# Residual joints of a fused two-layer network on one NeuronCore: norms and the neighbouring product tiles computed in two token halves

## The chip, the cores and the metric

One NeuronCore of one Trainium2 chip. The metric is the device time in microseconds (us) of one execution; the median of several executions is compared.

## The reference

The whole program is a stack of a hybrid mixer layer with cross-attention, a second layer with an attention and recurrence block, a short-convolution mixer, and gated feed-forward blocks, on 512 tokens of width 1024, all in float32. What matters here is the joint between two products of the second part of the stack. With y the output of a projection (1024 features x 512 tokens), h the residual stream, g, g' and s learned or conditioned vectors of 1024 features:

```
h = h + y * rsqrt(mean(y*y) + eps) * g        # first norm, added to the residual
n = h * rsqrt(mean(h*h) + eps) * g' + s       # second norm, input of the next product
z = W_next @ n
```

The means run over the 1024 features of each token. Tokens don't mix here, so any split over tokens is exact. There are four such joints, after the projections ab_out, down_1, sc_out and down_2; after the last one there is only the first line, and h is stored as the result.

## The kernel before

Activations lie feature-major: 128 features on the partitions, KT = 8 feature tiles, 512 tokens along the free axis. A product is computed one output tile of 128 features at a time over all 512 tokens. Each k-step of a tile (one feature tile of the input) is three matmuls in `passes` (lines 393 to 395), because weights and inputs are both split into a rounded high part and a low rest: high x high, high x low, low x high. ab_out has 16 k-steps a tile, down_1 and down_2 have 22, sc_out has 8. Four PSUM banks take the output tiles in turn.

The program is written by hand, engine by engine; each stage gives every engine's queue a list of instructions, and semaphores order them across engines. The weights of a tile come by DMA from SyncE into a ring of six slots; VectorE makes the high part (L344) and the low part (L346), which needs the high slot of the tile three before to be free (`split_until`, `split_weights`).

`plain_product` is the product ahead of a joint. ScalarE squares each output tile from PSUM (L2699) and copies it to y (L2701); GpSimd adds up the squares of the first seven tiles (L419).

`edge` is the joint. TensorE sums the squares over the partitions with a matrix of ones (L473, L476: four blocks of 128 tokens, 128 equal columns each), ScalarE takes the root (L496), VectorE the reciprocal (L518), and TensorE spreads the result over the partitions (`spread_root`, L465). VectorE then scales y (L530) and adds it to h (L534), tile by tile over 512 tokens; ScalarE squares the new h (L508), TensorE sums (L487). After the eighth tile come root, reciprocal and spread again. Then for each tile VectorE scales h (L541), ScalarE adds the shift and rounds it to the high part (L513), and VectorE makes the low part (L547). In between TensorE does `keep_busy` matmuls (L656) into a bank nobody reads: 11, then one after each of seven sums, then 8.

`product` of the next stage takes its first two tiles together (`lead=2`): for each k-step it waits for that tile's low part (`inputs_ready`), then does the three matmuls of tile 0 and of tile 1. The third tile begins when both are done. Behind the joints up_1, sc_in and up_2 follow; behind the last, `store_output` sends each finished tile of h to memory by a DMA from SyncE's queue (L3552). The joint before ab_in is another function, `double_edge`, and the one into up_0 belongs to `ffn_up` and `residual_product`.

Of the kernel before, what the change touches and what calls it, by code (L numbers as in the profile page):

```python
# [32 lines left out]
P = 128  # L33
T = 512
# [187 lines left out]
class Kernel:  # L222
# [126 lines left out]
    def product(self, pe, name, rhs, width, evacuated, between=None, inputs_ready=None, lead=1, banks_free=None,  # L349
                beside=None, upto=None, ready_from=0):  # L350
# [5 lines left out]
        for k in range(kt if lead > 1 else 0):  # L356
            if inputs_ready is not None:
                pe.wait_ge(inputs_ready, k + 1)
            for j in range(lead):
                if k == 0:  # L360
                    if banks_free is not None:
                        pe.wait_ge(banks_free[0], banks_free[1] - PRODUCT_BANKS + j + 1)
                    pe.wait_ge(self.weights_split, first + j + 1)
                last = self.passes(self.psum[:, j % PRODUCT_BANKS, 0:width], first + j, k, rhs(k), k == 0, k == kt - 1)
                if k == kt - 1:
                    last.then_inc(self.weights_used, 1)
            if beside is not None:
                beside(k)
# [18 lines left out]

    def passes(self, out, i, k, x, first, last):
# [11 lines left out]


# [48 lines left out]

def edge(k, name, before, first_gain, gain=None, shift=None, then=None, y=None):
# [3 lines left out]
    squared, added, out = (before.signals[s] for s in ("squared", "added", "out"))  # L455
    summed, rooted, inverted, spread, renewed, resquared, counted, scaled, shifted, steps, done = (
        k.sem(f"{name}_{s}") for s in ("summed", "rooted", "inverted", "spread", "renewed", "resquared", "counted",
                                       "scaled", "shifted", "steps", "done"))
    SUMS, SPREAD = 4, 2
    ones = k.const("ones")  # L460

    def spread_root(pe, i):
        pe.wait_ge(inverted, i + 1)
        for c in range(TT):
            last = nc.tensor.matmul(k.psum[:, SPREAD + i, c * P:(c + 1) * P],  # L465
                                    k.roots[:, i, c:c + 1].broadcast_to([P, P]), k.const("ident"),
                                    start=True, stop=True)
        last.then_inc(spread, 1)

    def tensor(pe):  # L470
        pe.wait_ge(added, KT - 1)
        for c in range(TT):
            nc.tensor.matmul(k.psum[:, SUMS + c, 0:P], k.sum_sq[:, c * P:(c + 1) * P], ones, start=True, stop=False)  # L473
        pe.wait_ge(squared, KT)
        for c in range(TT):
            last = nc.tensor.matmul(k.psum[:, SUMS + c, 0:P], k.squares[:, (KT - 1) % 2, c * P:(c + 1) * P],  # L476
                                    ones, start=False, stop=True)
        last.then_inc(summed, 1)
        spread_root(pe, 0)
        if gain is None:  # L480
            return
        pe.wait_ge(out, KT - 2)
        keep_busy(k, pe, 11)
        for j in range(KT):
            pe.wait_ge(resquared, j + 1)
            for c in range(TT):
                last = nc.tensor.matmul(k.psum[:, SUMS + c, P:2 * P], k.squares[:, j % 2, c * P:(c + 1) * P], ones,  # L487
                                        start=(j == 0), stop=(j == KT - 1))
            last.then_inc(counted, 1)
            if j < KT - 1:  # L490
                keep_busy(k, pe, 1)
        spread_root(pe, 1)
        keep_busy(k, pe, 8)
# [5 lines left out]
    def scalar(act):  # L499
        act.wait_ge(summed, 1)  # L500
        root(act, 0)
        if gain is None:
            return
# [18 lines left out]
    def vector(dve):  # L522
# [13 lines left out]
        if gain is None:  # L536
            return
# [3334 lines left out]
```

## Time and profile before

| | |
|---|---|
| median of 3 runs | 2417.52 us (2414.93 to 2419.92) |
| the profiled execution's own time | 2420.88 us |
| its span, first to last instruction | 2419.1 us |
| mean granted TensorE clock | 0.973 of full speed |
| busy: TensorE matmul, VectorE, ScalarE, GpSimd | 97%, 68%, 27%, 8% of the span |
| matmuls L393 to L395, all products | 722.1 + 712.1 + 712.0 us (inputs in n), 280 us each (inputs in the hidden buffers) |
| read from memory | 247.97 MB, 103 GB/s over the span |

A busy share says how much of the span an engine had an instruction under way. Matmuls overlap: one that is shown with 0.39 us starts 0.23 us after the one before. In the view in order of time a row has the start, the duration, the engine, the line of the code, the operation with output and inputs, and in brackets how long the engine stood idle and what released it. "x8" means eight instructions merged in one row. A float32 matmul of the sums and spreads is two instructions.

### The profile page before, as it was taken

Reading aid. Unit: us, or ns where it says so; the run is one execution under the profiler, and the core shown is the slowest. Engines: PE = TensorE matmul, PEld = TensorE weight load, DVE = VectorE, ACT = ScalarE, POOL = GpSimd, SP = SyncE. Lnnn points to the kernel's source line nnn. Section 1 sums busy time; section 2 is a strip of 40 time slices with the busy share of each in tenths; the row PEclk is TensorE's granted clock in tenths of the full one; section 3 lists DMA queues with packets and bytes.
Section 4 is the critical chain, followed back from the end, with each engine's and each line's share of the span. In section 5 each row is a group of like instructions: output and inputs, shape, how many; then the busy total and the mean of one; then the engine's idle time right before and its main releaser. Section 6 shows DMA issues by size and latency. Waiting matters only on the chain.

```text
span 2419.1 us, 35289 instructions
## 1 busy us (share of the span) xinstructions
PE 2335.3 (97%) x14624; PEld 1898.2 (78%) x14624; DVE 1651.3 (68%) x2569; ACT 663.9 (27%) x1200; POOL 183.2 (8%) x179
## 2 busy tenths in 40 slices
PE   8998879999999999999989999999999999999997
PEld 6886668878888888887756788888888888888886
DVE  6674366756888865559788777666667886666653
ACT  2321253022211201324768413222102113222200
POOL 0001222001000011003211010000010000000000
PEclk9999579999999999999999999999999999999998
DMA  4220003412222453322200361232562451322341
GB/s 183 79 79 2 21 3 122 158 52 88 96 96 96 135 204 130 107 81 92 88 1 2 138 219 62 98 100 97 197 214 104 182 186 63 102 96 96 127 141 64
DMA packets 71728, 253.94 MB, mean 105 GB/s; under 512 B 8560, under 2 KB 8848, under 8 KB 71056
## 3 DMA queue, kind: packets, MB, share of 16 engines
q1 hardware_dynamic: 71280, 251.14, 30.4%
q8 instruction: 116, 1.90, 0.3%
q10 hardware_dynamic: 288, 0.54, 0.1%
q14 instruction: 44, 0.36, 0.0%
HBM read 247.97 MB, written 2.10 MB: 103 GB/s over the span
## 4 chain that ended last, share of the span: by engine, by line
PE 47%; DVE 3%; issue 0%; ACT 0%; POOL 0%; DVEq 0%; POOLq 0%
PE psum L393 14%; PE psum L394 14%; PE psum L395 13%; PE psum L3362 1%; PE psum L487 1%; PE psum L3349 1%; PE psum L3384 1%; DVE scratch L3440 1%; DVE scratch L3416 1%; PE psum L656 0%; PE psum L3376 0%; PE psum L465 0%; DVE h L534 0%; DVE n L530 0%; PE psum L476 0%
## 5 line engine op out<-in xcount | busy, mean ns | idle before, releaser
L393 PE MATMUL psum<-rounded_n,rounded_high 128*128 128x512 f32 x1824 | 722.1, 396 | 8.0 <-DVE rounded_ring L346 4.6
L394 PE MATMUL psum<-rounded_n_low,rounded_high 128*128 128x512 f32 x1824 | 712.1, 390 | 0.0
L395 PE MATMUL psum<-rounded_n,rounded_ring 128*128 128x512 f32 x1824 | 712.0, 390 | 0.0
L346 DVE TENSOR_TENSOR rounded_ring<-ring,rounded_high 128x1024 fp32r<-128x1024 f32 (+1 forms) x360 | 448.4, 1246 | 43.5 <-ACT rounded_high L329 31.5
L393 PEld LDWEIGHTS psum<-rounded_n,rounded_high 128*128 128x128 f32 x1824 | 343.9, 189 | 86.6 <-issue 7.4
L394 PEld LDWEIGHTS psum<-rounded_n_low,rounded_high 128*128 128x128 f32 x1824 | 344.1, 189 | 74.2 <-issue 3.9
L395 PEld LDWEIGHTS psum<-rounded_n,rounded_ring 128*128 128x128 f32 x1824 | 343.7, 188 | 72.1
L344 DVE CAST rounded_high<-ring 128x1024 fp32r<-128x1024 f32 (+1 forms) x347 | 250.4, 722 | 188.3 <-PE psum L395 177.9
L393 PE MATMUL psum<-rounded_arena,rounded_high 128*128 128x512 f32 x720 | 280.2, 389 | 0.0
L395 PE MATMUL psum<-rounded_arena,rounded_ring 128*128 128x512 f32 x720 | 280.1, 389 | 0.0
L394 PE MATMUL psum<-rounded_arena,rounded_high 128*128 128x512 f32 x720 | 280.1, 389 | 0.0
L2617 DVE SCALAR_TENSOR_TENSOR scratch<-arena,vecs,scratch 128x512 f32<-128x512 f32 x88 | 65.9, 748 | 162.8 <-ACT scratch L2604 162.8
L393 PEld LDWEIGHTS psum<-rounded_arena,rounded_high 128*128 128x128 f32 x720 | 135.1, 188 | 28.3 <-issue 0.2
L395 PEld LDWEIGHTS psum<-rounded_arena,rounded_ring 128*128 128x128 f32 x720 | 135.1, 188 | 28.1
L394 PEld LDWEIGHTS psum<-rounded_arena,rounded_high 128*128 128x128 f32 x720 | 135.1, 188 | 27.9
L2598 ACT COPY arena<-psum 128x512 f32<-128x512 f32 x88 | 51.7, 587 | 351.2 <-PE psum L395 351.2
L2604 ACT ACTIVATE scratch<-arena,vecs 128x512 f32<-128x512 f32 x88 | 63.8, 725 | 188.4 <-DVE arena L2638 186.9
L2699 ACT ACTIVATE scratch<-psum 128x512 f32<-128x512 f32 x32 | 19.2, 600 | 317.4 <-PE psum L395 317.4
L419 POOL TENSOR_TENSOR sum_sq<-sum_sq,scratch 128x512 f32<-128x512 f32 x38 | 59.9, 1575 | 288.4 <-ACT scratch L2699 242.2
L416 POOL COPY sum_sq<-scratch 128x512 f32<-128x512 f32 x6 | 4.7, 786 | 955.4 <-ACT scratch L2699 820.0
L993 DVE CUSTOM_DVE_ANT_0 arena<-arena 128x1024 f32<-128x1024 f32 x48 | 61.9, 1333 | 13.4 <-DMA arena<-in_mod_w 13.4
L993 DVE CUSTOM_DVE_ANT_0 n_low<-n_low 128x1024 f32<-128x1024 f32 x48 | 56.7, 1221 | 19.9 <-DMA n_low<-in_mod_w 19.9
(507 smaller groups left out, 2798.3 us busy)
## 6 DMA issues: line engine op xcount, KB each, us to landing
ring<-in_w_up SPq DMA_DIRECT2D x132, 512.0 KB, 3.6
ring<-in_w_down SPq DMA_DIRECT2D x48, 512.0 KB, 3.5
n_low<-in_mod_w SPq DMA_DIRECT2D x48, 512.0 KB, 5.8
arena<-in_mod_w SPq DMA_DIRECT2D x48, 512.0 KB, 5.3
ring<-in_w_ab_in SPq DMA_DIRECT2D x37, 512.0 KB, 3.6
ring<-in_w_mix_in SPq DMA_DIRECT2D x31, 512.0 KB, 3.6
ring<-in_w_sc_in SPq DMA_DIRECT2D x24, 512.0 KB, 5.7
ring<-in_w_down SPq DMA_DIRECT2D x24, 384.0 KB, 3.0
```

The costliest lines, as they stand in the source:

```text
L344: nc.vector.tensor_copy(self.rounded(high), raw).then_inc(self.weights_rounded, 1)
L346: nc.vector.tensor_tensor(self.rounded(raw), raw, self.rounded(high), ALU.subtract).then_inc(self.weights_split, 1)
L393: self.nc.tensor.matmul(out, w_high, x_high, start=first, stop=False)
L394: self.nc.tensor.matmul(out, w_high, x_low, start=False, stop=False)
L395: return self.nc.tensor.matmul(out, w_low, x_high, start=False, stop=last)
L419: nc.gpsimd.tensor_tensor(total, total, sq, ALU.add).then_inc(added, 1)
L487: last = nc.tensor.matmul(k.psum[:, SUMS + c, P:2 * P], k.squares[:, j % 2, c * P:(c + 1) * P], ones, start=(j == 0), stop=(j == KT - 1))
L993: k.nc.vector.tensor_tensor_reduce(out=self.tiles[:, i % 3], in0=self.tiles[:, i % 3], in1=self.cond, scale=1.0, scalar=0.0, op0=ALU.mult, ...
L2598: nc.scalar.copy(x, k.psum[:, j % PRODUCT_BANKS, :]).then_inc(out, 1)
L2604: nc.scalar.activation(dst, x, ACT.Copy, scale=taps[:, col:col + 1]).then_inc(tapped, 1)
L2617: link(nc.vector.scalar_tensor_tensor(dst, src[:, 0:T], taps[:, col:col + 1], dst, ALU.mult, ALU.add))
L3349: last = nc.tensor.matmul(k.psum[:, 2 * (m % 2) + s, at * P:(at + nk) * P], k.z[rows, NQT + p, i * P:(i + 1) * P], k.z[rows, (KS, KW)[b] + ...
```

## The change

- **Last tile in halves.** `plain_product` computes tiles 0 to 6 as before. The last tile is computed by `last_tile` inside `edge`: all k-steps for tokens 0 to 255 into one bank, then all k-steps for tokens 256 to 511 into another. ScalarE evicts each half by itself (`evict`). In the stream of the second half, behind k-step 2, TensorE sums the first half's squares, and behind k-step 6 it spreads their root; from k-step 13 on, the sums of the second norm go out at every other step.
- **Both norms in halves.** All of `edge` runs for half 0 and then for half 1. The sums of squares have one output column now (`one`) instead of 128. `keep_busy` matmuls are fewer: two at every other of the last sums (8 for sc_out, 4 for ab_out, none for the down products), then three and three.
- **Five sums on GpSimd.** For feature tiles 0, 2, 3, 5 and 6 the sum h + y is done by GpSimd; VectorE keeps 1, 4 and 7.
- **The next product's first two tiles in halves.** `product` runs its lead for tokens 0 to 255 over all eight k-steps, then for 256 to 511. While it does the first half, VectorE updates h for half 1 between the scalings of half 0, and TensorE takes the sums of half 1 between the k-steps (`beside`).
- `early`, `late` and `lag` set where the second half's root and updates stand: early 0, 4, 8 and lag 0, 0, 2 for 8, 16 and 22 k-steps.
- The weight splits for the next product's first three tiles, all ahead of the first reciprocal before, are spread over the joint.
- The store has 16 DMAs of half a tile instead of 8.

The diff, cut (new lines and the lines around them; sums, spreads, roots and evictions keep their form at half the tokens):

```diff
@@ Kernel.product
+        for h in range(halves if lead > 1 else 0):
+            cols = tokens(h) if halves > 1 else slice(0, width)
+            for k in range(kt):
+                if inputs_ready is not None:
+                    pe.wait_ge(inputs_ready, kt * h + k + 1)
+                for j in range(lead):
+                    if h == 0 and k == 0:
+                        if banks_free is not None:
+                            pe.wait_ge(banks_free[0], banks_free[1] - PRODUCT_BANKS + j + 1)
+                        pe.wait_ge(self.weights_split, first + j + 1)
+                    x = [part[:, cols] for part in rhs(k)]
+                    last = self.passes(self.psum[:, j % PRODUCT_BANKS, cols], first + j, k, x, k == 0, k == kt - 1)
+                    if h == halves - 1 and k == kt - 1:
+                        last.then_inc(self.weights_used, 1)
+                if beside is not None:
+                    beside(kt * h + k)
...
+    def last_tile(self, pe, name, rhs, evacuated, first_half, meanwhile):
+        n_out, kt = PRODUCTS[name]
+        j, first = n_out - 1, self.first_tile[name] + (n_out - 1) * self.chunks(name)
+        for h in range(2):
+            pe.wait_ge(evacuated, j + h - PRODUCT_BANKS + 1)
+            out = self.psum[:, (j + h) % PRODUCT_BANKS, tokens(h)]
+            for kk in range(kt):
+                i = first + kk // SLOT_KT
+                if h == 0 and kk % SLOT_KT == 0:
+                    pe.wait_ge(self.weights_split, i + 1)
+                x = [part[:, tokens(h)] for part in rhs(kk)]
+                last = self.passes(out, i, kk % SLOT_KT, x, kk == 0, kk == kt - 1)
+                if h == 0 and kk == kt - 1:
+                    last.then_inc(first_half, 1)
+                if h == 1:
+                    if kk % SLOT_KT == SLOT_KT - 1 or kk == kt - 1:
+                        last.then_inc(self.weights_used, 1)
+                    meanwhile(kk)
...
+def tokens(h):
+    return slice(h * T // 2, (h + 1) * T // 2)
...
@@ edge
+POOL_ADDS = (0, 2, 3, 5, 6)
+    SUMS, RESUMS = 4, 6
+    SPREAD, RESPREAD = (3, 5), (7, 4)
+    one = k.const("ones")[:, 0:1]
+    kt = PRODUCTS[product][1]
+    early = 8 if kt > 16 else 4 if kt > 8 else 0
+    late = early == KT
+    lag = 2 if late else 0
...
+    def resums(pe, h, j):
+        pe.wait_ge(resquared, KT * h + j + 1)
+        for c in pieces(h):
+            last = nc.tensor.matmul(k.psum[:, RESUMS, c:c + 1], k.squares[:, j % 2, c * P:(c + 1) * P], one,
+                                    start=(j == 0 and c == 2 * h), stop=(j == KT - 1 and c == 2 * h + 1))
+        last.then_inc(counted, 1)
...
+        counts = []
+        def meanwhile(kk):
+            if kk == 2:
+                sums(pe, 0)
+            if kk == 6:
+                spread_root(pe, 0)
+            if gain is not None and kk >= 13 and kk % 2 == 1:
+                resums(pe, 0, len(counts))
+                counts.append(kk)
+        k.last_tile(pe, product, rhs, out, halved, meanwhile)
         if gain is None:
+            sums(pe, 1)
+            spread_root(pe, 1)
             return
         pe.wait_ge(out, KT - 2)
+        for j in range(len(counts), early):
+            resums(pe, 0, j)
+        if not late:
+            sums(pe, 1)
+        for j in range(early, KT):
+            if j % 2 == 0:
+                keep_busy(k, pe, 2)
+            resums(pe, 0, j)
+        if late:
+            keep_busy(k, pe, 3)
+            spread_again(pe, 0)
+            sums(pe, 1)
+        else:
+            spread_root(pe, 1)
+            keep_busy(k, pe, 3)
+            spread_again(pe, 0)
+        keep_busy(k, pe, 3)
+        pe.wait_ge(out, KT + 1)
...
+    def beside(pe):
+        def step(x):
+            if late and x == 0:
+                spread_root(pe, 1)
+            if lag + 2 <= x < KT:
+                resums(pe, 1, x - lag - 2)
+            if x == KT - 1:
+                for j in range(KT - lag - 2, KT):
+                    resums(pe, 1, j)
+                spread_again(pe, 1)
+        return step
...
+        def square(h, j):
+            updated(act, h, j)
+            if KT * h + j >= 2 and j >= 2:
+                act.wait_ge(counted, KT * h + j - 1)
+            nc.scalar.activation(k.squares[:, j % 2, tokens(h)], k.h[:, j, tokens(h)], ACT.Square
+                                 ).then_inc(resquared, 1)
+        def second_half():
+            evict(act, 1)
+            act.wait_ge(summed, 2)
+            root(act, SUMS, 0, 1, rooted)
+        def raise_high(h, j):
+            act.wait_ge(scaled, KT * h + j + 1)
+            nc.scalar.activation(k.rounded(k.n[:, j, tokens(h)]), k.n_low[:, j, tokens(h)], ACT.Identity,
+                                 bias=shift[:, j:j + 1]).then_inc(shifted, 1)
         act.wait_ge(summed, 1)
+        root(act, SUMS, 0, 0, rooted)
         if gain is None:
+            second_half()
             return
         for j in range(KT):
+            if j == early:
+                second_half()
+            square(0, j)
         act.wait_ge(counted, KT)
+        root(act, RESUMS, 1, 0, rerooted)
+        if late:
+            second_half()
         for j in range(KT):
+            raise_high(0, j)
+            if j >= lag + 1:
+                square(1, j - lag - 1)
+        for j in range(KT - lag - 1, KT):
+            square(1, j)
+        act.wait_ge(counted, 2 * KT)
+        root(act, RESUMS, 1, 1, rerooted)
+        for j in range(KT):
+            raise_high(1, j)
...
+    def pool(pool):
+        for h in range(2):
+            for j in POOL_ADDS:
+                pool.wait_ge(stepped, KT * h + j + 1)
+                nc.gpsimd.tensor_tensor(k.h[:, j, tokens(h)], k.h[:, j, tokens(h)], y[:, j, tokens(h)], ALU.add
+                                        ).then_inc(renewed_pool, 1)
...
+        def update(h, j):
+            at = tokens(h)
+            nc.vector.scalar_tensor_tensor(y[:, j, at], y[:, j, at], first_gain[:, j:j + 1],
+                                           k.psum[:, SPREAD[h], at], ALU.mult, ALU.mult).then_inc(stepped, 1)
+            if j not in POOL_ADDS:
+                dve.wait_ge(stepped, KT * h + j + 1)
+                nc.vector.tensor_tensor(k.h[:, j, at], k.h[:, j, at], y[:, j, at], ALU.add).then_inc(renewed, 1)
...
+        invert(0, 0, rooted, inverted)
+        dve.wait_ge(spread, 1)
         dve.wait_ge(out, KT)
         for j in range(KT):
+            update(0, j)
         if gain is None:
+            invert(0, 1, rooted, inverted)
+            dve.wait_ge(spread, 2)
+            dve.wait_ge(out, KT + 1)
+            for j in range(KT):
+                update(1, j)
             return
+        following = k.first_tile[then]
+        k.split_until(dve, following + 1)
+        if not late:
+            invert(0, 1, rooted, inverted)
+        invert(1, 0, rerooted, reinverted)
+        k.split_until(dve, following + 2)
+        dve.wait_ge(respread, 1)
+        for j in range(KT + lag):
+            if j < KT:
+                scale(0, j)
+            if late and j == 0:
+                invert(0, 1, rooted, inverted)
+            if j == lag:
+                dve.wait_ge(spread, 2)
+                dve.wait_ge(out, KT + 1)
+            if j >= lag:
+                update(1, j - lag)
+            if 1 <= j <= KT:
+                low_part(0, j - 1)
+        if lag == 0:
+            low_part(0, KT - 1)
+        k.split_until(dve, following + 3)
+        invert(1, 1, rerooted, reinverted)
+        dve.wait_ge(respread, 2)
         for j in range(KT + 1):
             if j < KT:
+                scale(1, j)
             if j >= 1:
+                low_part(1, j - 1)
...
@@ store_output
+        for h in range(2):
+            for j in range(KT):
+                before.signals["updated"](sp, h, j)
+                sp.dma_start(k.dram["out"][:, j, tokens(h)], k.h[:, j, tokens(h)]).then_inc(k.stored, 16)
```

## Rows read from the trace of the kernel before

**Rows 1.** the page's line of busy time of each engine

```profile
PE 2335.3 (97%) x14624; PEld 1898.2 (78%) x14624; DVE 1651.3 (68%) x2569; ACT 663.9 (27%) x1200; POOL 183.2 (8%) x179
```

**Rows 2.** TensorE in order of time, sc_out to up_2 (start us, us, line)

```profile
2016.12 0.39 PE L393 MATMUL psum<-rounded_arena,rounded_high 128*128 128x512 f32 x1
...
2021.56 1.05 PE L473 MATMUL psum<-consts,sum_sq 128*128 128x128 f32 x8
...
2022.45 1.12 PE L476 MATMUL psum<-consts,scratch 128*128 128x128 f32 x8
...
2042.47 0.50 PE L393 MATMUL psum<-rounded_n,rounded_high 128*128 128x512 f32 x1 [0.60 <-DVE rounded_n_low L547]
...
2053.51 0.39 PE L393 MATMUL psum<-rounded_n,rounded_high 128*128 128x512 f32 x1
```

**Rows 3.** the same at the other joints: first matmuls of last, third tiles

```profile
1435.41 0.39 PE L393 MATMUL psum<-rounded_arena,rounded_high 128*128 128x512 f32 x1
...
1478.26 0.39 PE L393 MATMUL psum<-rounded_n,rounded_high 128*128 128x512 f32 x1
...
1811.46 0.39 PE L393 MATMUL psum<-rounded_arena,rounded_high 128*128 128x512 f32 x1
...
1858.36 0.39 PE L393 MATMUL psum<-rounded_n,rounded_high 128*128 128x512 f32 x1
...
2386.71 0.39 PE L393 MATMUL psum<-rounded_arena,rounded_high 128*128 128x512 f32 x1
```

**Rows 4.** VectorE in order of time in the joint after sc_out

```profile
2025.33 0.75 DVE L530 SCALAR_TENSOR_TENSOR n<-n,mod_cols,psum 128x512 f32<-128x512 f32 x1 [1.25 <-PE psum L465]
...
2035.79 0.69 DVE L534 TENSOR_TENSOR h<-h,n 128x512 f32<-128x512 f32 x1
...
2040.12 1.41 DVE L541 SCALAR_TENSOR_TENSOR n_low<-h,mod_cols,psum 128x512 f32<-128x512 f32 x2 [1.25 <-PE psum L465]
```

**Rows 5.** TensorE in order of time: memory keys, and up_0's sums

```profile
425.12 0.28 PE L393 MATMUL psum<-rounded_upper,rounded_high 128*128 128x256 f32 x1
...
425.24 0.28 PE L394 MATMUL psum<-rounded_upper,rounded_high 128*128 128x256 f32 x1
...
595.70 0.95 PE L2557 MATMUL psum<-consts,sum_sq 128*128 128x1 f32 x8
```

**Rows 6.** half-width instructions on VectorE, ScalarE and GpSimd (min/median/max ns)

```profile
396.10 0.87 DVE L689 SCALAR_TENSOR_TENSOR rounded_upper<-upper,vecs,rounded_upper 128x256 fp32r<-128x256 f32 x2
...
384.41 0.49 ACT L672 ACTIVATE rounded_upper<-upper,vecs 128x256 fp32r<-128x256 f32 x1
...
L685 POOL TENSOR_TENSOR scratch<-scratch x7: 737/740/1533, 380.8 to 386.8; 128x256 f32<-128x256 f32 x7
```

**Rows 7.** GpSimd adds and the VectorE instructions beside them, in order of time

```profile
2011.55 1.29 POOL L419 TENSOR_TENSOR sum_sq<-sum_sq,scratch 128x512 f32<-128x512 f32 x1 [4.15 <-ACT scratch L2699]
...
2011.67 2.25 DVE L346 TENSOR_TENSOR rounded_ring<-ring,rounded_high 128x1024 fp32r<-128x1024 f32 x1
...
2022.55 1.22 DVE L346 TENSOR_TENSOR rounded_ring<-ring,rounded_high 128x1024 fp32r<-128x1024 f32 x1
...
561.17 2.09 POOL L419 TENSOR_TENSOR sum_sq<-sum_sq,scratch 128x512 f32<-128x512 f32 x1
...
562.03 0.68 DVE L2513 TENSOR_TENSOR h<-h,psum 128x512 f32<-128x512 f32 x1
```

**Rows 8.** DMA issues of the span's end: KB each, median us to landing

```profile
out_t<-h SPq DMA_DIRECT2D x8, 256.0 KB, 2.0
```

**Rows 9.** stretches: us, busy PE, PEld, DVE, ACT, POOL, granted clock, DMA

```profile
2021.80:2042.60 20.80, 19.06 (x149) 17.15 (x148) 15.51 (x24) 7.98 (x14) 0.00 (x0) 1.00 0.07 26
...
948.00:960.00 12.00, 9.50 (x75) 8.79 (x74) 9.25 (x18) 3.25 (x6) 0.00 (x0) 1.00 0.80 298
...
1052.00:1054.00 2.00, 2.00 (x6) 1.52 (x6) 1.66 (x3) 0.52 (x2) 0.00 (x0) 0.50 0.14 31
```

**Rows 10.** TensorE in order of time ahead of 1052

```profile
1046.78 4.14 PE L2853 MATMUL psum<-rest,arena 64*128 64x32 f32 x62
```

More of the change, by code:

```diff
@@ L459, in edge @@
[L459 to L466, printed above, removed]
+    squared, added, out, halved = (before.signals[s] for s in ("squared", "added", "out", "halved"))
+    product, rhs, evict = (before.signals[s] for s in ("product", "rhs", "evict"))
@@ new lines, in sums, with spread_root @@
+    def sums(pe, h):
+        if h == 0:
+            pe.wait_ge(added, KT - 1)
+        pe.wait_ge(squared, KT + h)
+        for c in pieces(h):
+            col, at = k.psum[:, SUMS, c:c + 1], slice(c * P, (c + 1) * P)
+            nc.tensor.matmul(col, k.sum_sq[:, at], one, start=True, stop=False)
+            last = nc.tensor.matmul(col, k.squares[:, (KT - 1) % 2, at], one, start=False, stop=True)
+        last.then_inc(summed, 1)
+    def spread_root(pe, h):
+        pe.wait_ge(inverted, h + 1)
+        pe.wait_ge(out, KT + h)
+        for c in pieces(h):
+            last = nc.tensor.matmul(k.psum[:, SPREAD[h], c * P:(c + 1) * P],
+                                    k.roots[:, 0, c:c + 1].broadcast_to([P, P]), k.const("ident"),
@@ L467, in spread_root @@
                                     start=True, stop=True)
         last.then_inc(spread, 1)
-    def tensor(pe):
[L471 to L479, printed above, removed]
+    def resums(pe, h, j):
+        pe.wait_ge(resquared, KT * h + j + 1)
+        for c in pieces(h):
+            last = nc.tensor.matmul(k.psum[:, RESUMS, c:c + 1], k.squares[:, j % 2, c * P:(c + 1) * P], one,
+                                    start=(j == 0 and c == 2 * h), stop=(j == KT - 1 and c == 2 * h + 1))
+        last.then_inc(counted, 1)
@@ new lines, in spread_again @@
+    def spread_again(pe, h):
+        pe.wait_ge(reinverted, h + 1)
+        for c in pieces(h):
+            last = nc.tensor.matmul(k.psum[:, RESPREAD[h], c * P:(c + 1) * P],
+                                    k.roots[:, 1, c:c + 1].broadcast_to([P, P]), k.const("ident"),
+                                    start=True, stop=True)
+        last.then_inc(respread, 1)
+    def tensor(pe):
+        counts = []
[8 more added lines that the diff above has]
+        k.last_tile(pe, product, rhs, out, halved, meanwhile)
@@ L2570, in tensor @@
         else:
-            k.product(pe, name, k.normed, T, out, inputs_ready=before.signals["done"], lead=2)
+            k.product(pe, name, k.normed, T, out, inputs_ready=before.signals["done"], lead=2, halves=2,
+                      beside=before.signals["beside"](pe))
     def scalar(act):
@@ L3504, in tensor @@
     def tensor(pe):
-        k.product(pe, "sc_in", k.normed, T, out, inputs_ready=before.signals["done"], lead=2)
+        k.product(pe, "sc_in", k.normed, T, out, inputs_ready=before.signals["done"], lead=2, halves=2,
+                  beside=before.signals["beside"](pe))
     def scalar(act):
```

135 lines of the change are left out of this document (59 added, 76 removed).

## The prediction, made before the change was built or run

> **What bounds the kernel now.** I read the page first: TensorE is busy 97% of the span, VectorE 68%, GpSimd 8% [rows 1]. Time can therefore leave only where TensorE does no product. The instructions in order of time around the joint after sc_out show such a place: the first matmul of the last tile starts at 2016.12 and the products stop at 2021.56; from then until 2042.47 TensorE does only sums, spreads and stand-in matmuls, and the third tile of up_2 starts at 2053.51. The joint, from the last tile to the third tile, takes 37.4 us [rows 2]. The same stretch takes 42.9 us after ab_out and 46.9 us after down_1, and from the last tile of down_2 to the end of the span it is 32.4 us [rows 3]. These four are all that the change touches.
>
> Inside a joint VectorE is the clock: eight pairs of a scale (0.74) and an add (0.69), one pair each 1.38 us, from 2025.33 to 2036.48. Then follow square, sums, root, reciprocal and spread, 3.6 us, until the second scaling starts at 2040.12, and 2.35 us more until the first matmul [rows 4, 2]. After that two tiles take 11.0 us at 0.23 us a matmul, TensorE bound, because VectorE hands over a tile of the norm in 1.32 us and TensorE wants 1.36.
>
> **Prices of the new pieces.** A 256-column matmul of the same kind starts every 0.120 us, against 0.227 for 512, so two halves cost 0.013 us more than one whole [rows 5]. A sum with one output column is two instructions of 0.10 us each (eight in 0.95 us with 0.25 for the last one's end), since its weights are still 128 wide; eight wide ones went by in 0.89 [rows 5, 2]. So narrowing the sums saves nearly nothing. A matmul that follows a wait takes 0.50 us instead of 0.39, and I charge the same 0.10 to the product matmul after a group of sums [rows 2]. VectorE at half width takes 0.48 us and starts the next after 0.40; ScalarE up to 0.49; a GpSimd add 0.74 [rows 6]. Halves thus cost VectorE 0.80 us for what took 0.66.
>
> By the Trainium skill (TensorE: Matmul & The Clock Gate, Back-to-back issue gap) an isolated matmul at full clock costs N/2.4 + 2.5 ns, 0.109 us for 256 columns. The rows say 0.120, and they decide; by the page's figure the sum below would be an estimated 5 us lower, about no change.
>
> GpSimd and VectorE also stop each other. A VectorE subtract with both inputs in SBUF that takes 1.22 us alone took 2.25 beside a GpSimd add and ended 1.08 us after it; another GpSimd add took 2.09 because it first waited for such a subtract, and while it ran a VectorE add that reads PSUM kept its 0.68 [rows 7]. So I charge waits to the instructions with two inputs in SBUF: the three adds left on VectorE, the low parts and the weight splits. The norm's scalings read PSUM as their second input; they also read a gain, which the add of the row did not, so their bounds are no wait and a full one (0.6 us, five per half), and I take none, by the nearest row.
>
> **The joint after sc_out, step by step**, in us from the first matmul of the last tile:
> - First half, 24 x 0.120 = 2.9. In the second half's stream come three k-steps (1.1), the sums (0.9), four k-steps (1.4) and the spread (0.6). VectorE's updates start at 7.0, against 9.2 before. Only 2.2 us are won, because the spread is written behind k-step 6.
> - Eight scalings at 0.40 and three adds at 0.38: 4.3, plus some 0.5 per VectorE add spent behind GpSimd: 5.8. First update done at 12.8.
> - Square, eight sums of 0.4 that queue on TensorE with the second half's sums and root, three stand-ins, spread: 3.3. Scaling of half 0 starts at 16.1 (before: 24.0). The lead's first matmul comes at 18.7.
> - Then VectorE does, per tile, scale, update of half 1 and low part: 8 x 1.20 + 3 x 0.38 = 10.7. ScalarE adds to it: its square of half 1 waits for a sum that TensorE does only after a lead step, and the next high part queues behind that square. I take 12.5 (a period of 2.9 us for two tiles). Done at 28.6. TensorE needs 5.8 + 3.2 for leads and sums here, so it waits.
> - Last squares, sums, root, spread again: 4.0; the third weight split (1.9: 0.7 for the high part, 1.2 for the low [rows 7]) lies inside. Scaling of half 1 starts at 32.6.
> - 8 x 0.80 = 6.4, plus 0.6 for the first and 0.9 for TensorE behind the last. Third tile at 40.5.
>
> So 40.5 against 37.4: 3.1 us **longer**. Half the joint starts 8 us sooner, but VectorE's work, now with 24 more starts, a second statistics chain and the ScalarE loop, is strung out while TensorE has only half tiles to fill in.
>
> After ab_out the same steps give 45.8 (start of updates 9.8 instead of 14.5; the second half's square and root sit in the middle of the first's squares; a weight split of 1.9 on VectorE lies after the first root): +3.0. After down_1 (22 k-steps; sums go out at every other k-step; lag 2; two splits on VectorE between the updates and the scaling) I get 49.2: +2.3.
>
> **The end.** First half 7.9, updates from 12.0 to 17.8 under the second half, which ends at 17.3; second chain 3.0; updates 20.3 to 26.1; the last store lands 2.0 after its issue [rows 8]: 28.2 against 32.4, 4.2 us **shorter**. The 16 stores have 1 KB per partition instead of 2 KB; half of them are out before the last updates. If the smaller rows halve the rate, 1 us of the gain goes.
>
> **Sum:** +3.1 +3.0 +2.3 -4.2 = +4.2, say +4.3 us. The profiled execution took 2420.88 us (span 2419.1), 3.4 above the median 2417.52 of the three runs; the difference carries over to the median: **2421.8 us**. Bounds: without the ScalarE loop (-1.7) and without waits behind GpSimd (-2) each inner joint comes to about zero, -5 in all; with scalings that wait for GpSimd too, +15 and more.
>
> **Rivals.** (1) TensorE's clock falls in the joints. It is 1.00 through the joint now, with 128-column sums and stand-ins in every gap [rows 9]. In the change sums are one column wide, stand-ins fall from 26 matmuls to 14, 10 and 6, and TensorE waits 2 us or so at two places. For the case: at 1052 to 1054 the clock was at half, just after 4.1 us in which TensorE was busy without a gap, but with matmuls of 32 columns [rows 9, 10]. Against: in the joint before ab_in, at 948 to 960, TensorE idled 2.5 us of 12, with wide sums, and the clock stayed at 1.00 [rows 9]. It decides once a lead step with its sum (1.1 us) doubles, past VectorE's 1.55. At half clock six matmuls of 512 columns went by in 2 us instead of nine [rows 9]; a few such microseconds, with the sums in the chain, I price at 2 to 3 us per inner joint, +6 to +9 on the sum: 2429 us.
>
> The Trainium skill (TensorE: Matmul & The Clock Gate, Part 1) says that the throttled state is the default and activity releases it. By that alone the thinner joint would run in part at half clock; rows 9 give its price.
>
> (2) The halves hide what they are meant to: ScalarE keeps up, VectorE's step is 1.34, the statistics chains shrink with width. Each inner joint then gains about 2 us, with the end -4.2: -10, 2407 us. For it: TensorE has slack in every step; against: the VectorE sum alone (5 + 10.7 + 6.4 + 3.3 + 4.0) already gives 37 us.
>
> (3) The GpSimd adds cost more than the three VectorE waits (a slow handover to ScalarE, whose squares run in order): +1 per joint, 2425 us.
>
> **How the numbers follow.** My sum (+4.3, between -1 and +9) has 0.45, on both sides of the bound: a measurement of this kernel tells 0.2%, 4.8 us, from no change. The clock has 0.25, the gain 0.20, the GpSimd case 0.10. Slower: 0.21 of the first, all of the second but a little, most of the third, 0.47. Same: 0.33. Faster: 0.20. The range takes in the gain at its low end and the clock at its high end: 2407 to 2433.
>
> **What would show it.** Right: updates of half 0 start about 7, 10 and 12 us after the last tile's first matmul; in the first lead half TensorE waits at nearly every step for VectorE's low part, which waits for ScalarE; third tiles at 40.5, 45.8 and 49.2; the tail 4 us shorter. Rival 1: granted clock under 1.00 in the windows of the joints. Rival 2: third tiles under 36, 41 and 45. I am wrong at the root if VectorE's step in the first lead half is near 1.2 us, or if scalings from PSUM are stretched by GpSimd.

## The result: 1.1% slower, and the profile after

The changed kernel takes 2443.28 us (median of 4 runs, 2439.26 to 2448.65) against 2416.70 for the kernel before in the same session: ratio 1.0108, 95% interval 1.0094 to 1.0121. That is 26 us slower; the prediction had 4 us slower, and its range ended at 2433. The profiled execution took 2440.57 us (span 2438.8), near the fast end of its four. In the sessions below the kernel before had medians of 2416.2, 2420.3 and 2416.8 us, its executions spread over 10 to 12 us in each session; the ratios rest on all of them, and so differ a little from the quotient of two medians.

| | before | after |
|---|---|---|
| median | 2416.70 us | 2443.28 us |
| profiled execution, span | 2420.88, 2419.1 us | 2440.57, 2438.8 us |
| mean granted clock | 0.973 | 0.964 |
| joint ab_out to up_1 (forecast) | 42.9 us | 52.8 us (45.8) |
| joint down_1 to sc_in (forecast) | 46.9 us | 52.1 us (49.2) |
| joint sc_out to up_2 (forecast) | 37.4 us | 47.5 us (40.5) |
| last tile of down_2 to the end (forecast) | 32.4 us | 28.5 us (28.2) |

A joint runs, as in the prediction, from the first matmul of a product's last tile to the first of the next product's third tile. These are TensorE's rows of after for it, in order of time (start us, duration us, engine, line); they answer to [rows 2, 3]:

```profile
1433.68 0.28 PE L416 MATMUL psum<-rounded_arena,rounded_high 128*128 128x256 f32 x1
...
1486.49 0.40 PE L416 MATMUL psum<-rounded_n,rounded_high 128*128 128x512 f32 x1
...
1819.71 0.28 PE L416 MATMUL psum<-rounded_arena,rounded_high 128*128 128x256 f32 x1
...
1871.77 0.40 PE L416 MATMUL psum<-rounded_n,rounded_high 128*128 128x512 f32 x1
...
2029.56 0.28 PE L416 MATMUL psum<-rounded_arena,rounded_high 128*128 128x256 f32 x1
...
2077.09 0.40 PE L416 MATMUL psum<-rounded_n,rounded_high 128*128 128x512 f32 x1
...
2410.32 0.28 PE L416 MATMUL psum<-rounded_arena,rounded_high 128*128 128x256 f32 x1
```

The end came as forecast. The three inner joints are 25 us longer than before where 8 were forecast, and what lies between two joints has not moved (1486.49 to 1819.71 is 333.2 us; before, 1478.26 to 1811.46, the same). The busy line of the page, against [rows 1], shows an odd thing: TensorE is busier by 14 us, though its products are the same.

```profile
PE 2349.1 (96%) x14876; PEld 1928.4 (79%) x14876; DVE 1658.8 (68%) x2648; ACT 675.3 (28%) x1263; POOL 213.8 (9%) x219
```

The stretches of the joint after sc_out say why. Columns: length, busy time of PE, PEld, DVE, ACT and POOL, then the granted clock, DMA share and GB/s; [rows 9] showed 1.00 through the same joint before.

```profile
2037.00:2039.00 2.00, 1.57 (x12) 1.41 (x12) 1.97 (x5) 1.06 (x5) 1.21 (x2) 1.00 0.59 154
2039.00:2041.00 2.00, 1.96 (x12) 1.96 (x13) 1.97 (x5) 1.12 (x3) 1.25 (x3) 0.68 0.27 109
2041.00:2043.00 2.00, 2.00 (x11) 2.00 (x11) 1.42 (x3) 0.46 (x2) 1.09 (x2) 0.50 0.00 0
2049.00:2051.00 2.00, 2.00 (x12) 2.00 (x11) 0.00 (x0) 0.00 (x0) 0.00 (x0) 0.50 0.00 0
2057.00:2059.00 2.00, 2.00 (x19) 2.00 (x17) 1.67 (x5) 0.82 (x2) 0.42 (x1) 1.00 0.00 0
2065.00:2067.00 2.00, 1.33 (x11) 1.16 (x11) 0.59 (x2) 0.68 (x2) 0.00 (x0) 1.00 0.00 0
2067.00:2069.00 2.00, 0.57 (x4) 0.28 (x2) 1.21 (x3) 0.88 (x2) 0.00 (x0) 0.51 0.01 4
2071.00:2073.00 2.00, 2.00 (x12) 2.00 (x10) 2.00 (x6) 1.30 (x3) 0.00 (x0) 0.50 0.00 0
2073.00:2075.00 2.00, 2.00 (x15) 2.00 (x15) 1.37 (x5) 0.74 (x2) 0.00 (x0) 0.79 0.00 0
```

TensorE's clock falls to half (1.2 GHz) from about 2040 to 2057, and again from 2067 to 2074. The other two joints show two falls as well. Half clock takes 24, 17 and 24 us of the three joints; before, none.

TensorE in order of time at the first fall:

```profile
2038.24 0.69 PE L824 MATMUL psum<-consts 128*128 128x128 f32 x4
2039.04 1.26 PE L537 MATMUL psum<-consts,scratch 128*128 128x1 f32 x8
2040.16 1.20 PE L824 MATMUL psum<-consts 128*128 128x128 f32 x4
2041.15 1.71 PE L537 MATMUL psum<-consts,scratch 128*128 128x1 f32 x8
2042.72 1.20 PE L824 MATMUL psum<-consts 128*128 128x128 f32 x4
2043.71 1.71 PE L537 MATMUL psum<-consts,scratch 128*128 128x1 f32 x8
```

L537 sums the new squares, one column wide; L824 are the stand-ins. Both are counted in instructions here, two to a matmul. A round of two feature tiles' sums (x8) and two stand-ins (x4) starts every 2.56 us (2041.15 to 2043.71). VectorE in the same joint, to be held against the steps of the prediction:

```profile
2036.48 0.87 DVE L659 SCALAR_TENSOR_TENSOR n<-n,mod_cols,psum 128x256 f32<-128x256 f32 x2 [1.52 <-PE psum L529]
...
2041.42 0.95 DVE L663 TENSOR_TENSOR h<-h,n 128x256 f32<-128x256 f32 x1
...
2051.21 0.48 DVE L668 SCALAR_TENSOR_TENSOR n_low<-h,mod_cols,psum 128x256 f32<-128x256 f32 x1 [2.74 <-PE psum L544]
```

Counted from 2029.56, updates start at 6.9 (forecast 7.0) and are done at 12.8 (12.8), sums beside GpSimd taking 0.66 to 0.96 us. Up to here every number fits. The scaling starts at 21.7, forecast 16.1: the chain of squares, sums, root and spread, all of it through TensorE, took 8.8 us (from the end of the last sum, 2042.37) in place of 3.3.

### The profile page after: what moved, and what is told of

Same layout as the page of the kernel before. It is cut to its first block, busy times and chain, and to the rows that moved or that the text cites. A ratio compares the mean times of both kernels' runs of the same rounds, so it can differ in the third digit from the quotient of the medians.

```text
span 2438.8 us, 36028 instructions
## 1 busy us (share of the span) xinstructions
PE 2349.1 (96%) x14876; PEld 1928.4 (79%) x14876; DVE 1658.8 (68%) x2648; ACT 675.3 (28%) x1263; POOL 213.8 (9%) x219
## 4 chain that ended last, share of the span: by engine, by line
PE 46%; DVE 3%; issue 1%; ACT 0%; POOL 0%; ACTq 0%; POOLq 0%
PE psum L416 14%; PE psum L418 13%; PE psum L417 13%; PE psum L3547 1%; PE psum L3534 1%; PE psum L3569 1%; PE psum L537 1%; DVE scratch L3625 1%; DVE scratch L3601 1%; PE psum L824 0%; PE psum L3561 0%; DVE n L659 0%; DVE rounded_n_low L674 0%; DVE n_low L668 0%; PE psum L529 0%
## 5 line engine op out<-in xcount | busy, mean ns | idle before, releaser
L416 PE MATMUL psum<-rounded_n,rounded_high 128*128 128x512 f32 (+1 forms) x1872 | 737.8, 394 | 17.9 <-DVE rounded_n_low L674 8.9
L417 PE MATMUL psum<-rounded_n_low,rounded_high 128*128 128x512 f32 (+1 forms) x1872 | 725.4, 388 | 0.0
L418 PE MATMUL psum<-rounded_n,rounded_ring 128*128 128x512 f32 (+1 forms) x1872 | 725.3, 387 | 0.0
L416 PEld LDWEIGHTS psum<-rounded_n,rounded_high 128*128 128x128 f32 x1872 | 358.3, 191 | 96.7 <-issue 11.3
L417 PEld LDWEIGHTS psum<-rounded_n_low,rounded_high 128*128 128x128 f32 x1872 | 358.7, 192 | 72.1 <-issue 3.6
L418 PEld LDWEIGHTS psum<-rounded_n,rounded_ring 128*128 128x128 f32 x1872 | 358.1, 191 | 70.6
L416 PE MATMUL psum<-rounded_arena,rounded_high 128*128 128x512 f32 (+1 forms) x788 | 293.2, 372 | 0.0
L417 PE MATMUL psum<-rounded_arena,rounded_high 128*128 128x512 f32 (+1 forms) x788 | 292.1, 371 | 0.0
L418 PE MATMUL psum<-rounded_arena,rounded_ring 128*128 128x512 f32 (+1 forms) x788 | 292.1, 371 | 0.0
L417 PEld LDWEIGHTS psum<-rounded_arena,rounded_high 128*128 128x128 f32 x788 | 148.4, 188 | 25.7
L416 PEld LDWEIGHTS psum<-rounded_arena,rounded_high 128*128 128x128 f32 x788 | 148.4, 188 | 25.5 <-issue 0.2
L418 PEld LDWEIGHTS psum<-rounded_arena,rounded_ring 128*128 128x128 f32 x788 | 148.4, 188 | 25.4
L2767 ACT COPY arena<-psum 128x512 f32<-128x512 f32 x88 | 51.7, 587 | 351.4 <-PE psum L418 351.4
```

The source lines that it names most:

```text
L416: self.nc.tensor.matmul(out, w_high, x_high, start=first, stop=False)
L417: self.nc.tensor.matmul(out, w_high, x_low, start=False, stop=False)
L418: return self.nc.tensor.matmul(out, w_low, x_high, start=False, stop=last)
L2767: nc.scalar.copy(x, k.psum[:, j % PRODUCT_BANKS, :]).then_inc(out, 1)
```

## The experiments

Theory **W**: the clock falls because the sums became one column wide. **G**: it falls because TensorE waits too much in the statistics. **S**: the clock is no cause; the chain of halves is this long. Since the time ahead of the first joint differs by several us from one execution to the next (that joint starts between 1427 and 1436 us in the kernels after, the later the more half clock the trace has ahead of 1400 us: 92 us in more_busy, 116 us in wide_sums), joints are compared one by one, and the ratio says whether the sum agrees.

**wide_sums.** The kernel after, its sums 128 columns wide again (cut; the root then reads every 128th column):

```diff
-            nc.tensor.matmul(col, k.sum_sq[:, at], one, start=True, stop=False)
+            nc.tensor.matmul(col, k.sum_sq[:, at], ones, start=True, stop=False)
...
-            last = nc.tensor.matmul(k.psum[:, RESUMS, c:c + 1], k.squares[:, j % 2, c * P:(c + 1) * P], one,
+            last = nc.tensor.matmul(k.psum[:, RESUMS, c * P:(c + 1) * P], k.squares[:, j % 2, c * P:(c + 1) * P], ones,
```

> The kernel after, with one edit: every sum over the partitions in the joints (the sums of the product's squares and those of the new h) takes 128 equal columns of ones again, as before, in place of one column; same instructions, same order, same stand-ins. Theory W (width): TensorE's clock falls to half in the inner joints because the matmuls there are one column wide; with wide ones it keeps the clock at least for the first of the two falls, the three inner joints come back from 52.8, 52.1 and 47.5 us to about 46 to 49, and the time to 2420 to 2428. Theory G (gaps): the clock falls because TensorE waits too much in the statistics part, whatever the width of its matmuls: the joints stay within 1.5 us of what they are, the time within 2438 to 2446. Theory S (schedule): the clock is no cause at all, the chain of the halves itself is this long: as G, with the clock up.

Measured: 2422.55 us, ratio to before 1.0024 (1.0011 to 1.0038). The joints are 47.0, 49.2 and 40.8 us, the end 28.5. Half clock is left in two places, 3.4 us each, behind the wait ahead of the lead of the first two joints. W holds: by the ratios some 20 of the 26 us are back, in the joints and the end of the profiled executions 15 (180.8 to 165.6 us).

**more_busy.** Stand-ins instead, sums still narrow (`if j % 2 == 0` dropped; 3 to 6, twice a joint):

> The kernel after, one-column sums kept, with more stand-in matmuls on TensorE: two ahead of each sum of new squares in place of two ahead of every second one, and six in place of three before and after the spreading of the second root. Theory G (gaps): the clock stays up or falls later, joints shorter by 3 us or more each, time 2425 to 2434. Theory W (width): stand-ins are 128 wide, so they help some: the first fall comes later or goes, time 2430 to 2438. Theory S (schedule): nothing gained, and the stand-ins stand in the way: 2441 to 2447.

Measured: 2435.08 us, 1.0079 (1.0062 to 1.0096); joints 52.7, 53.3 and 43.7 us, half clock 17, 14 and 3 us. Stand-ins help one joint of three; joints and end are together 2.8 us shorter than in the kernel after, while the ratios say 7. They don't undo what the narrow sums do.

**before_one_column.** The kernel before, and nothing but `ones` cut to one column, in both sums (the diff shows the second):

```diff
-                nc.tensor.matmul(k.psum[:, SUMS + c, P:2 * P], k.squares[:, j % 2, c * P:(c + 1) * P], ones,
+                nc.tensor.matmul(k.psum[:, SUMS + c, P:P + 1], k.squares[:, j % 2, c * P:(c + 1) * P], one,
```

> The kernel before, with one edit: the sums in the joints one column wide in place of 128, its 26 stand-ins per joint kept. Theory W (width): part of what held the clock is gone, the clock falls in at least one of the inner joints and the time goes up by 3 to 10 us. Theories G and S: within 1.5 us of before.

Measured: 2433.89 us, 1.0075 (1.0061 to 1.0089): 18 us slower, where W gave 3 to 10. The inner joints take 47.1, 52.0 and 43.8 us, 16 more than before, the end 32.8. The order of work and all 26 stand-ins are those of before. The stretches of the joint after sc_out in this kernel:

```profile
2033.80:2034.80 1.00, 1.00 (x12) 1.00 (x10) 0.16 (x1) 0.00 (x0) 0.00 (x0) 0.97 0.05 21
2034.80:2038.20 3.40, 3.40 (x19) 3.40 (x18) 3.30 (x6) 1.26 (x2) 0.00 (x0) 0.51 0.00 0
2038.20:2041.40 3.20, 3.20 (x32) 3.20 (x30) 3.13 (x5) 1.26 (x2) 0.00 (x0) 1.00 0.00 0
2041.40:2058.60 17.20, 16.63 (x78) 16.51 (x78) 7.88 (x14) 4.73 (x8) 0.00 (x0) 0.50 0.00 1
2058.60:2060.00 1.40, 1.40 (x7) 1.12 (x6) 1.40 (x4) 0.80 (x2) 0.00 (x0) 0.99 0.00 0
```

and TensorE in order of time in it:

```profile
2034.44 4.25 PE L656 MATMUL psum<-consts 128*128 128x128 f32 x22
2038.52 0.95 PE L487 MATMUL psum<-consts,scratch 128*128 128x1 f32 x8
2039.33 0.47 PE L656 MATMUL psum<-consts 128*128 128x128 f32 x2
2039.64 0.95 PE L487 MATMUL psum<-consts,scratch 128*128 128x1 f32 x8
...
2042.14 1.71 PE L487 MATMUL psum<-consts,scratch 128*128 128x1 f32 x8
```

The clock falls first behind the 16 narrow instructions that sum the product's squares, a wait of 0.57 us and a wide spread. It is back when 11 stand-ins (22 instructions, wide) have gone by. It falls again at about 2041.5, though TensorE has been busy without a gap since 2033.4, by then in rounds of 8 narrow instructions and 2 of a stand-in, and stays down for 17 us, into the first matmul of up_2. The joints hold 14, 17 and 21 us of half clock; before, with the same instructions and TensorE busy for 19.06 of 20.8 us ([rows 9]), none. So width alone does it, in either order of work. G and S fall as main causes.

**resums_wide.** The many sums over the new h wide (64 instructions a joint), the 16 over the product's squares narrow:

> The kernel after with 128 columns in the sums of the new h alone (32 matmuls a half), the 8 matmuls a half over the product's squares left one column wide. Theory W: the fall goes with the count of narrow matmuls near each other, and these are the many: nearly all comes back, 2422 to 2427. If the few narrow ones beside the last tile matter as much, it stays above 2430.

Measured: 2428.38 us, 1.0027 (1.0014 to 1.0041); joints 46.9, 49.2 and 40.8 us, as in wide_sums. The median lies just above W's 2427; six of the ten executions are near 2429, four at 2419 to 2422, and the ratio is that of wide_sums within its interval. The few narrow sums, with products around them, cost nothing.

**wide_busy_wait.** wide_sums, with stand-ins in the one wait where it still lost the clock:

```diff
-        keep_busy(k, pe, 3)
+        keep_busy(k, pe, 9)
         pe.wait_ge(out, KT + 1)
```

> The kernel after with wide sums, and nine in place of three stand-ins ahead of the next product's first matmul in each inner joint, where wide_sums still showed TensorE waiting 1.9 to 3.5 us and, in two of the three joints, 3.4 us of half clock just behind that wait. Theory G (what is left of the fall comes from that wait): no half clock in the joints, the first two inner joints about 1 us shorter each, 2419 to 2422. Theory W alone (width was all): nothing more to gain, or the stand-ins get in the way: 2422 to 2425.

Measured: 2422.29 us, 1.0020 (1.0008 to 1.0033); no half clock in any joint; joints 46.0, 49.2 and 40.9 us, end 28.6. The first joint is 1 us shorter, the second not at all. This is the change at full clock, the case that the prediction's sum had worked out. The stretch of its joint after sc_out, 1.00 being the granted clock, and TensorE in it:

```profile
2016.60:2057.40 40.80, 35.82 (x281) 33.55 (x280) 29.04 (x63) 17.36 (x43) 9.13 (x11) 1.00 0.08 27
```

```profile
2016.56 0.28 PE L416 MATMUL psum<-rounded_arena,rounded_high 128*128 128x256 f32 x1
...
2027.59 1.06 PE L538 MATMUL psum<-consts,scratch 128*128 128x128 f32 x8
2028.48 0.61 PE L825 MATMUL psum<-consts 128*128 128x128 f32 x4
2028.93 1.06 PE L538 MATMUL psum<-consts,scratch 128*128 128x128 f32 x8
...
2035.54 0.35 PE L416 MATMUL psum<-rounded_n,rounded_high 128*128 128x256 f32 x1 [0.64 <-issue]
...
2057.42 0.40 PE L416 MATMUL psum<-rounded_n,rounded_high 128*128 128x512 f32 x1
```

and VectorE in it:

```profile
2023.48 0.87 DVE L660 SCALAR_TENSOR_TENSOR n<-n,mod_cols,psum 128x256 f32<-128x256 f32 x2 [1.41 <-PE psum L530]
...
2028.42 0.96 DVE L664 TENSOR_TENSOR h<-h,n 128x256 f32<-128x256 f32 x1
...
2032.93 0.48 DVE L669 SCALAR_TENSOR_TENSOR n_low<-h,mod_cols,psum 128x256 f32<-128x256 f32 x1 [1.10 <-PE psum L545]
...
2045.00 0.48 DVE L675 SCALAR_TENSOR_TENSOR rounded_n_low<-n_low,mod_cols,rounded_n 128x256 fp32r<-128x256 f32 x1 [0.79 <-ACT rounded_n L618]
...
2049.55 0.87 DVE L669 SCALAR_TENSOR_TENSOR n_low<-h,mod_cols,psum 128x256 f32<-128x256 f32 x2 [0.80 <-PE psum L545]
```

From the first matmul of the last tile: updates start at 6.9 (forecast 7.0), done at 12.8 (12.8); scaling of half 0 at 16.4 (16.1), its last low part done at 28.9 (28.6); scaling of half 1 at 33.0 (32.6); third tile at 40.9 (40.5). A round of sums and stand-ins (x8 and x4) starts every 1.34 us (2027.59 to 2028.93), against 2.56 in the kernel after, where the sums do 1/128 of the columns.

**wide_no_gpsimd.** `POOL_ADDS = ()`, sums wide:

> The kernel after with wide sums (as in wide_sums, so that the clock is out of the question), and all eight sums h plus y of each half on VectorE, none on GpSimd. Theory A (GpSimd helps by what it takes from VectorE, five of eight sums of 0.43 us less what VectorE waits for it): the schedule of the prediction, worked through again without GpSimd, makes the inner joints 1.6, 1.5 and 2.1 us longer and the end 1.1, so 6 us more than wide_sums (about 2428.5). Theory B (the stretched sums, 0.66 to 0.96 us beside GpSimd, eat the gain): within 2 us of wide_sums.

Measured: 2433.11 us, 1.0058 (1.0042 to 1.0073), against 1.0024 for wide_sums. Joints 49.7, 51.7 and 44.7 us, end 29.3: longer than in wide_sums by 2.7, 2.5, 3.9 and 0.8, together 9.9 where 6 were expected. With VectorE slower, TensorE waits more, and half clock is back (10, 3 and 10 us); the surplus is in joints where it is. In those joints the run doesn't part the two. The joint after down_1, with 3.4 us of half clock in both kernels, is 2.5 us longer (forecast 1.5), and the end is 0.8 longer (forecast 1.1). So theory A holds: GpSimd pays for what it takes over. The end at 29.3, against 32.4 before, also says that the halves bring 3.0 of its 3.9 us and GpSimd the rest.

**before_no_stand_ins.** Plain waiting, priced in the kernel before: its 26 stand-ins a joint gone.

> The kernel before, sums 128 wide, without its 26 stand-in matmuls in each inner joint (11, 7 times 1, and 8); nothing else changed. It prices a clock lost to plain waiting, in the schedule that is known. If waiting alone takes the clock: the sums of squares and the spreading double while they are on the chain (some 1 to 2 us a joint), and the next product starts at half clock (7 us of half clock cost about 3.5 us): 4 to 6 us a joint, 12 to 18 in all, about the 17.6 us that narrow sums alone cost in before_one_column. The rival, that stand-ins do little there: within 3 us of before.

Measured: 2421.18 us, 1.0013 (1.0002 to 1.0024): 3 us, at the rival's bound, not 12 to 18. Stretches of the joint after sc_out:

```profile
2024.00:2026.00 2.00, 0.68 (x7) 0.49 (x5) 1.25 (x2) 0.00 (x0) 0.00 (x0) 1.00 0.03 12
2026.00:2028.00 2.00, 1.00 (x5) 1.03 (x6) 1.97 (x4) 1.02 (x2) 0.00 (x0) 0.79 0.00 0
2028.00:2030.00 2.00, 2.00 (x12) 2.00 (x11) 1.93 (x4) 0.87 (x2) 0.00 (x0) 0.50 0.00 0
2030.00:2032.00 2.00, 2.00 (x16) 1.98 (x16) 1.97 (x4) 0.87 (x2) 0.00 (x0) 0.85 0.00 0
```

The clock does fall, but it is back after some 3 us, while TensorE does nothing but wide sums. It falls a second time, for 7 us, behind a wait of 2.4 us ahead of up_2's first matmul:

```profile
2040.80:2047.60 6.80, 5.75 (x14) 4.50 (x15) 6.67 (x11) 3.76 (x6) 0.00 (x0) 0.50 0.00 0
```

The joints are 1.6, 1.7 and 2.7 us longer, and all of it lies behind that second fall: from the last tile to the next product's first matmul they take 31.8, 35.9 and 26.3 us, as before. The first falls (3, 7 and 3 us), beside VectorE's updates, cost nothing. So a lost clock costs little where it comes back soon or where another engine is the slower one; narrow sums keep it down.

**halved_end.** Only the last joint changed, the inner ones as before:

> The three inner joints as in the kernel before (whole tokens, wide sums, 26 stand-ins), and only the last one, behind the last product, in halves with its five sums on GpSimd as in the kernel after. The end took 28.5 us in the kernel after against 32.4 before, so every theory expects 4 us less than before, 0.998 of its time (about 2413 us), faster than both kernels. Above 2416 it would say that the end's gain hung on something in the inner joints.

Measured: 2413.10 us, 0.9984 (0.9971 to 0.9997). From up_2's first matmul to the end it is 372.7 us against 376.6: 3.9 us, as in the kernel after. Faster than both kernels.

**gpsimd_adds.** halved_end, and two sums of each whole joint on GpSimd, behind three scalings each:

```diff
+WHOLE_POOL_ADDS = (0, 3)
...
+        for group in ((0, 1, 2), (3, 4, 5), (6,), (7,)):
+            for j in group:
+                nc.vector.scalar_tensor_tensor(y[:, j, :], y[:, j, :], first_gain[:, j:j + 1], rstd,
+                                               ALU.mult, ALU.mult).then_inc(stepped, 1)
+            for j in group:
+                if j not in WHOLE_POOL_ADDS:
+                    dve.wait_ge(stepped, j + 1)
+                    nc.vector.tensor_tensor(k.h[:, j, :], k.h[:, j, :], y[:, j, :], ALU.add).then_inc(renewed, 1)
```

> As halved_end (inner joints whole, as before; the last joint in halves), and in the three inner joints two of the eight sums h plus y (tiles 0 and 3, 512 wide) on GpSimd, with VectorE's three scalings of tiles 0 to 2 and of 3 to 5 put one behind the other, so that they cover GpSimd's 1.29 us. VectorE then does 8 scalings and 6 sums in place of 8 and 8: 1.4 us less in each joint, 4 us less in all: 2409 us. Rival: the first new squares come 0.7 us later and the stand-ins no longer cover TensorE's wait, so that its clock falls: 2415 or more. Rival: GpSimd's sums hold up VectorE's by as much as they save: 2413.

Measured: 2410.45 us, 0.9968 (0.9955 to 0.9981), no half clock in an inner joint. From up_1 to sc_in and from sc_in to up_2 it is 1.3 and 1.2 us less than before (378.9 against 380.1, 193.9 against 195.1); the three joints take 41.6, 45.7 and 36.2 us, 3.7 less together. VectorE and GpSimd there, in order of time:

```profile
2016.90 2.06 DVE L810 SCALAR_TENSOR_TENSOR n<-n,mod_cols,psum 128x512 f32<-128x512 f32 x3 [1.25 <-PE psum L740]
2018.88 1.28 DVE L815 TENSOR_TENSOR h<-h,n 128x512 f32<-128x512 f32 x2
2020.09 2.06 DVE L810 SCALAR_TENSOR_TENSOR n<-n,mod_cols,psum 128x512 f32<-128x512 f32 x3
```

```profile
2017.73 1.28 POOL L795 TENSOR_TENSOR h<-h,n 128x512 f32<-128x512 f32 x1 [7.87 <-DVE n L810]
```

GpSimd's sum lies almost wholly beside scalings that read PSUM, and neither is stretched: it took 1.28 us, three scalings started every 0.66 us, two sums of VectorE every 0.6. Not all of the gain is GpSimd's. The updates take 9.2 us where they took 11.2 ([rows 4]): the two sums account for 1.2, the new order for 0.7, since before each sum started 0.78 us behind its own scaling, not 0.66. The chain behind the last sum then takes 0.7 longer (the scaling starts 4.3 us after it, before 3.6). The order by itself was not run.

**gpsimd_adds_six.** The same with six sums a half on GpSimd at the end:

> As gpsimd_adds, and in the last joint, the halved one, six of the eight sums of a half on GpSimd in place of five (tile 1 too). The schedule worked through gives 0.6 us less at the end if GpSimd's 0.73 us a sum still fit behind VectorE's scalings (0.9965 of before); if GpSimd has become the bound, or VectorE's two sums wait longer, the same as gpsimd_adds or worse by up to 1 us.

Measured: 2408.12 us, 0.9957 (0.9944 to 0.9971). The end is 0.5 us shorter (372.2 against 372.7), forecast 0.6, read from one execution of each; the two ratios' intervals overlap. Its ratio is the lowest of the study, some 10 us ahead of the kernel before.

## Why the prediction was wrong

**The end** was right: 28.2 forecast, 28.5 measured.

**The schedule of the inner joints** was right at full clock. It gave 45.8, 49.2 and 40.5 us, and wide_busy_wait has 46.0, 49.2 and 40.9. That covers the charges made from distant rows: 0.10 us behind a wait, the sums on VectorE held up by GpSimd, scalings from PSUM not held up, the loop through ScalarE (12.5 us for half 0's scaling to last low part, measured 12.5). The four together were forecast 4.3 us longer and came out 5.1 longer (164.6 us against 159.5), 4.8 by the ratio (2 to 8 by its interval). Halving the inner joints loses even with its clock whole.

**The clock** was wrong, in three steps.
- The term that failed is "Square, eight sums of 0.4 that queue on TensorE ...: 3.3" in the joint after sc_out. It took the sums at full clock, and was 8.8 us; at full clock, in wide_busy_wait, it is 3.55. After ab_out the same chain was 2.9 us longer than there, but after down_1, where half of these sums go out beside the last tile and the clock falls only later, it wasn't: the scaling of half 0 starts at 23.3 in the kernel after and at 23.5 in wide_busy_wait. With the end, the kernel after takes 180.8 us and wide_busy_wait 164.6: half clock cost 16 us in the profiled execution.
- The rival that named this had the right cause but the wrong price and place. It priced 2 to 3 us a joint. Measured, kernel after less wide_busy_wait: 6.8, 2.8 and 6.7 us. It was to decide "once a lead step with its sum doubles"; in the joint after sc_out the first lead half with its sums took no longer than at full clock (12.4 us from the scaling to the last low part, against 12.5), and 5.3 us went in the statistics chain of half 0, where every round of sums is on the path, and 1.6 us behind the second fall, in half 1's lead. After ab_out it was 2.9 there, 2.5 in half 1's chain and 1.7 in its lead. Only after down_1 did the first lead half stretch, 13.8 us for 12.5; half 1's lead took 2.1 more. Of the rival's three reasons (narrow sums, fewer stand-ins, waits) width brings nearly all: wide_sums has the same few stand-ins and waits, and 3, 3 and 0 us of half clock.
- Its chance, 0.25, was too low. [Rows 9, 10] had shown half clock behind 4.1 us of gapless matmuls of 32 columns, and I set against it a joint with waits but wide sums. That joint speaks of waits, not of width. "Narrowing the sums saves nearly nothing" was right for the issue time (0.10 against 0.11 us) and ended the thought too early: I asked what it saves, not what it costs.

**The other rivals** did not come about: at full clock the third tiles come at 40.9, 46.0 and 49.2, not under 36, 41 and 45, and the sums on GpSimd saved time. The terms set against rival 2 (5 + 10.7 + 6.4 + 3.3 + 4.0) add up to 29.4, not to 37; only with the 7.0 ahead of the updates do they reach 36.4. The low bound of the sum is by its own terms nearer -7 than -5. Neither slip enters the forecast.

What is not settled: the medians are 26 us apart, the profiled executions 20. Joints and end are 21 us longer there, and the first joint starts 2 us earlier; the profiled execution of before is 4 us above its median, that of after 3 below. The other executions of after had clocks from 0.958 to 0.965; how long the falls were in them isn't known.

## What to carry to other kernels

When work on TensorE is made narrower to save its columns, look at the granted clock before the busy share: the narrow form here had the same issue time and cost 18 us, in a kernel where nothing else was touched. Stand-ins held the clock across waits here; they didn't make up for narrow matmuls among them. Where a joint is bound by VectorE, splitting it into halves adds starts and a second statistics chain; here that paid only where nothing follows (the end). Handing VectorE's sums to GpSimd paid in the halves (9.9 us lost without it, part of it through the clock); in the whole joints it paid 1.2 us each, together with the new order of VectorE's instructions.

## What the runs showed that was not expected

- A clock can fall to half and stay there with TensorE busy without a gap: in before_one_column at about 2041.5, and 16.63 of 17.2 us busy while it stayed down, until 2052.4 with two instructions in ten 128 columns wide. The Trainium skill (TensorE: Matmul & The Clock Gate, Part 1) says that activity releases the throttle. In this case the busy share of the profile did not tell whether the clock would hold: it was 1.00 at this fall.
- Removing all stand-ins cost 3 us; making the sums narrow beside all stand-ins cost 18. With wide sums the stand-ins save little.
- A lost clock costs less than its length suggests: 27 us of half clock in the joints of before_no_stand_ins cost 3 us by the ratio and 6 by the stretches, 65 us in the kernel after some 16. It depends on what else is slow there: the first falls of before_no_stand_ins, beside VectorE's updates, cost nothing, the second ones, at the start of the next product, all of the 6 us.
